# Seven half products for the gate and up tiles of the third feed-forward stage, and its hidden tile on GpSimd

## The reference, cut to what matters

```python
D_FF = 2816
def swiglu(x, w_gate, w_up, w_down):
    return (jax.nn.silu(x @ w_gate) * (x @ w_up)) @ w_down
for i in range(DEPTH):
    h = h + 0.5 * swiglu(rmsnorm(h, norm_ffn1[i]), ffn1_w_gate[i], ffn1_w_up[i], ffn1_w_down[i])
    ...                      # mixer, second feed-forward
    gate = jax.nn.sigmoid(rmsnorm(h, norm_ple[i]) @ w_ple_gate[i])
    h = h + gate * (p[i] @ w_ple_proj[i])
```

## Time and profile before

| | us |
|---|---|
| median of 3 runs | 3317.61 (3317.11 to 3319.28) |
| profiled execution | 3314.88 |
| its span, first to last instruction | 3313.6 |
| gate and up of stage 2 | 1084.05 to 1324.40 in the span |
| down of stage 2 | 1324.40 to 1444.08 |

### The profile page before, as it was taken

How to read it: one execution, slowest core, us unless ns; L and a number is a source line. 1 busy time by engine, 2 the same in 40 slices (tenths; PEclk the granted TensorE clock), 3 DMA queues, 4 the chain that set the end, 5 groups by cost and what they waited for, 6 DMA issues and landing times. The chain is left out here.

```text
span 3313.6 us, 46922 instructions
## 1 busy us (share of the span) xinstructions
PE 3213.5 (97%) x20296; PEld 2465.6 (74%) x20296; DVE 1528.2 (46%) x2218; ACT 1067.6 (32%) x1594; POOL 308.9 (9%) x365
## 2 busy tenths in 40 slices
PE   9999999999999999999999999979999999989988
PEld 7888887888888888889788888768877888424332
DVE  5443456644435544332754434685567544301112
ACT  4222226432223322322632223553344323200001
POOL 1000131200001000000210001211111301100000
PEclk9999999999999999999999999999999999999999
DMA  4222441122233222333222222301010323899998
GB/s 145 102 90 90 145 145 40 39 102 89 90 97 109 100 95 90 96 107 109 84 89 102 98 88 91 113 20 50 3 65 20 105 99 126 337 427 425 425 427 345
DMA packets 62798, 448.77 MB, mean 135 GB/s; under 512 B 8704, under 2 KB 10368, under 8 KB 32640
## 3 DMA queue, kind: packets, MB, share of 16 engines
q1 hardware_dynamic: 62592, 445.76, 36.0%
HBM read 438.39 MB, written 2.10 MB: 133 GB/s over the span
## 5 line engine op out<-in xcount | busy, mean ns | idle before, releaser
L568 DVE TENSOR_TENSOR w_lo<-slot,w_hi 128x2048 fp32r<-128x2048 f32 (+4 forms) x243 | 487.3, 2005 | 331.5 <-ACT w_hi L559 329.3
L167 PE MATMUL bank<-xa,w_hi 128*128 128x512 f32 x1368 | 535.7, 392 | 2.0 <-DVE w_lo L3162 2.0
L168 PE MATMUL bank<-xa,w_hi 128*128 128x512 f32 x1368 | 532.4, 389 | 0.0
L169 PE MATMUL bank<-xa,w_lo 128*128 128x512 f32 x1368 | 532.3, 389 | 0.0
L559 ACT ACTIVATE w_hi<-slot 128x2048 fp32r<-128x2048 f32 (+4 forms) x243 | 406.1, 1671 | 335.5 <-PE bank L169 327.0
L167 PE MATMUL bank<-xb,w_hi 128*128 128x512 f32 x832 | 324.7, 390 | 0.8 <-DVE w_lo L568 0.7
L169 PE MATMUL bank<-xb,w_lo 128*128 128x512 f32 x832 | 323.7, 389 | 0.0
L168 PE MATMUL bank<-xb,w_hi 128*128 128x512 f32 x832 | 323.7, 389 | 0.0
L167 PEld LDWEIGHTS bank<-xa,w_hi 128*128 128x128 f32 x1368 | 256.7, 188 | 63.1 <-issue 5.4
L168 PEld LDWEIGHTS bank<-xa,w_hi 128*128 128x128 f32 x1368 | 256.8, 188 | 53.9 <-issue 1.2
L169 PEld LDWEIGHTS bank<-xa,w_lo 128*128 128x128 f32 x1368 | 256.8, 188 | 53.7
(11 more groups left out here) (508 smaller groups left out, 4863.8 us busy)
## 6 DMA issues: line engine op xcount, KB each, us to landing
slot<-in_w_gu SPq DMA_DIRECT2D x87, 1024.0 KB, 4.8
slot<-in_exp_gate SPq DMA_DIRECT2D x25, 2048.0 KB, 15.1
slot<-in_exp_up SPq DMA_DIRECT2D x24, 2048.0 KB, 15.3
slot<-in_exp_down SPq DMA_DIRECT2D x24, 2048.0 KB, 15.8
slot<-in_w_dn SPq DMA_DIRECT2D x64, 704.0 KB, 4.0
slot<-in_w_gate SPq DMA_DIRECT2D x24, 768.0 KB, 4.3
xe<-in_exp_up SPq DMA_DIRECT2D x8, 2048.0 KB, 13.1
xe<-in_exp_down SPq DMA_DIRECT2D x8, 2048.0 KB, 15.2
```

Of the source, the lines that this page charges most:

```text
L167: e.matmul(out, w[0], x[0], start=(j == 0), stop=False)
L168: e.matmul(out, w[0], x[1], start=False, stop=False)
L169: return e.matmul(out, w[1], x[0], start=False, stop=(j == n - 1))
L568: dve.e.tensor_tensor(lo, slot(k, b), hi.bitcast(F32), ALU.subtract).then_inc(L.up("w_lo", b))
```

## The change

In stage 2 the gate and up tile is a product of 2 x 2 blocks: rows are gate and up, the inner sum is cut in two halves of 4 feature tiles, the 512 tokens in two halves of 256. It is made from 7 products (numbered 1 to 7, run in the order 1, 5, 2, 6, 7, 3, 4) of 4 feature tiles x 3 passes over 256 tokens: 84 matmuls of 256 columns instead of 48 of 512. Each of the 7 has a weight of 512 columns that is a block or a sum of blocks; each is split by ACT and DVE, into a ring of 8. The sums of weights are made by adding DMAs that POOL issues, but for one by DVE. 2 MB and not 1 MB are read from HBM per tile. x needs differences of its blocks too (made in the ple stage). DVE puts the 7 results together (`four`), POOL multiplies silu(gate) and up, and the split into `hid` is made for hidden tiles 0 to 9 during the last tile and for 10 to 21 behind it. `rstd` of the up half is applied in the down step, by one more DVE operation per output tile. The diff, cut to its core:

```diff
+SEVEN_ORDER = (1, 5, 2, 6, 7, 3, 4)
...
+def seven_free(k, f, s):
+
+    if s < 8:
+        return ("w_used", k.first[f"gu{f}"] - (2 if s < 4 else 1))
+    return ("seven", f, s - 8 if s < 152 else s - 4)
...
+def pe_seven(k, f, nm):
...
+        pe.wait_ge(*L.at("comb_lo", f, s))
+        for j in range(4):
+            c, t = slice(SEVEN_X[p] * 256, SEVEN_X[p] * 256 + 256), slice(j * P, (j + 1) * P)
+            x_lo, x_hi = cols(k.sv.x[j][:2], c)
+            pe.wait_ge(*L.at(SEVEN_READY[p], nm, j))
+            e.matmul(out, hi[:, t], x_hi, start=(j == 0), stop=False)
+            e.matmul(out, hi[:, t], x_lo, start=False, stop=False)
+            last = e.matmul(out, lo[:, t], x_hi, start=False, stop=(j == 3))
+        last.then_inc(L.up("seven", f, s))
+
+    for m in range(FF):
+        for p in SEVEN_ORDER:
+            product(p, m)
+            if m == 0 and p == 6:
+                pe_norm(k, nm)
...
+def pool_comb(k, f, m):
+
+    pool, L, b = k.pool, k.led, k.first[f"gu{f}"] + m
+    pool.wait_ge(*L.at("w_in", b))
+    pool.e.dma_start(k.sv.raw[m % 3][:, 1536:2560], k.order[b][0][:, 3072:4096], accum_op=ALU.add).then_inc(
+        L.up(f"raw_sum{m % 3}", b, by=16, also=[("w_sum", b)]), 16)
+    pool.wait_ge(*L.at("w_sum", b))
+    pool.e.dma_start(k.sv.pairs[m % 3], seven_raw(k, 5, m), accum_op=ALU.add).then_inc(
+        L.up(f"raw_sum{m % 3}", f"{b}", by=16, also=[("w_sum2", b)]), 16)
...
+def pool_hidden(k, f, m):
...
+    pool.wait_ge(*L.at("silu", f, m))
+    pool.wait_ge(*L.at("up_right", f, m))
+    pool.wait_ge(*L.at("ends", f, m))
+    pool.e.tensor_tensor(sv.hidden[m].rearrange("p (a c) -> p a c", a=2), ups, gates, ALU.mult).then_inc(L.up("hid_pool", f, m))
...
+        if layer == 0 and i == KT - 1:
+            for p in (1, 5, 2, 6):
+                dve_comb(k, SEVEN_FFN, p, 0)
...
-            dve_norm(k, nx, i, gain, k.xa)
+            dve_seven_x(k, nx, i)
...
+    pool_comb(k, SEVEN_FFN, 0)
+    pool_comb(k, SEVEN_FFN, 1)
     pool_norm(k, "n4")
+    for m in range(FF):
+        if m + 2 < FF:
+            pool_comb(k, SEVEN_FFN, m + 2)
+        pool_hidden(k, SEVEN_FFN, m)
```

More of the change, by code:

```diff
@@ L44 @@
 SIGNALS = {kind: sem for sem, kinds in {
+    "mixer_sums": "ple_gate ple_proj gate2 pool_mix branch rot qk_sum qk_spread seven",
+    "mixer_curves": "class_hi v_out p_hi edge_hi raw_in qk_sq qk_root yr_hi gate2_sigmoid mg_hi h_scaled",
+    "mixer_vectors": "ple_scaled ple_gated qk_part qk_scaled qk_inv qk_scale root_part root_sum gate2_scaled branch_gated merge_add mg_lo yr_lo p_lo",
+    "seven_curves": "comb_hi first_part x_f32 x1_hi x5_hi x2_f32 x23_hi x674_hi",
+    "seven_vectors": "comb_lo comb_sum gate_left two_more rest up_right ends gate_ready x5_diff x1_lo x5_lo x7_diff x6_diff x4_diff x23_lo x674_lo",
     "rwkv_sums": "kk_sum kk_spread low ysum bonus_sum ysq_sum y_spread g_sum",
@@ L235, in __init__, with plan_seven, area, block @@
         self.rb = [rb[:, i * P:(i + 1) * P] for i in range(3)] if rb is not None else [a.buf(P, "den_inv") for _ in range(3)]
+def plan_seven(k):
+    m, made = Kernel(), []
+    def area(start, size):
+        a = Arena(k.nc, start, made)
+        a.end = start + size
+        return a
+    def block(a):
+        b = a.copy()
+        return (a.buf(7 * 256, "xc_lo", F32R), a.buf(7 * 256, "xc_hi", F32R), b.buf(7 * 256, "x_low"), b.buf(7 * 256, "x_high"))
+    def pair(a):
+        b = a.copy()
+        return (a.buf(512, "comb_hi", F32R), a.buf(512, "comb_lo", F32R), b.buf(512, "comb_full"), b.buf(512, "comb_full"))[:4]
+    slots, parts, x, z = 3432, 11624, 19816, 28008
+    a = area(x, 8192)
+    m.x = [block(a), block(a)]
+    m.pairs = [a.buf(512, "raw7") for _ in range(2)] + [area(2880, 512).buf(512, "raw7")]
+    a = area(z, 12800)
+    b = a.copy()
+    hid_lo, m.hidden = [a.buf(512, "hid7_lo", F32R) for _ in range(FF)], [b.buf(512, "hidden") for _ in range(FF)]
+    m.four = a.buf(1024, "four")
+    m.first, m.two = a.buf(256, "first_part"), a.buf(256, "two_part")
+    a = area(z + 12800, 7168)
+    hid_late = [a.copy()]
+    m.x += [block(a), block(a)]
+    b = hid_late[0]
+    late = [b.buf(512, "hid7_hi", F32R) for _ in range(12)]
+    assert b.at <= a.at
+    m.raw = [a.buf(5 * 512, "raw7") for _ in range(2)]
+    b = area(a.at - 5120, 5120)
+    early = [b.buf(512, "hid7_hi", F32R) for _ in range(10)]
+    m.hid = [(hi, lo) for hi, lo in zip(early[5:] + early[:5] + late, hid_lo)]
+    a = area(slots + 1536, 2560)
+    m.raw += [a.buf(5 * 512, "raw7")]
+    a = area(parts, 8192)
+    m.ring = [pair(a) for _ in range(8)]
+    return m
 def plan_memory(k):
@@ L645, in pe_idle, with seven_raw @@
     last.then_inc(L.up("idle", name))
+SEVEN_ORDER = (1, 5, 2, 6, 7, 3, 4)
+SEVEN_BANK = {1: "one", 5: "mid", 2: "two", 6: "six", 7: "mid", 3: "end", 4: "end"}
+SEVEN_FREE = {"one": "first_part", "mid": "up_right", "two": "gate_left", "six": "two_more", "end": "ends"}
+SEVEN_X = {1: 0, 5: 1, 2: 2, 3: 3, 6: 4, 7: 5, 4: 6}
+SEVEN_READY = {1: "x1_lo", 5: "x5_lo", 2: "x23_lo", 3: "x23_lo", 6: "x674_lo", 7: "x674_lo", 4: "x674_lo"}
+SEVEN_RAW = {1: 0, 2: 512, 4: 1024, 7: 1536, 5: 2048}
+def seven_raw(k, p, m):
+    return k.sv.pairs[m % 3] if p == 6 else k.sv.raw[m % 3][:, SEVEN_RAW[p]:SEVEN_RAW[p] + 512]
@@ new lines, in act_hid_hi, with dve_hid_lo @@
+def act_hid_hi(k, f, j):
+    act, L = k.act, k.led
+    hi, lo = k.sv.hid[j]
+    act.wait_ge(*L.at("hid_pool", f, j))
+    act.wait_ge(*(L.at("comb_lo", f, seven_turn(4, FF - 2 if j < 5 else FF - 1)) if j < 10 else L.at("seven", f, 7 * FF - 1)))
+    act.e.activation(hi, k.sv.hidden[j], ACT.Copy).then_inc(L.up("hid_hi", f, j))
+def dve_hid_lo(k, f, j):
+    dve, L = k.dve, k.led
+    hi, lo = k.sv.hid[j]
+    dve.wait_ge(*L.at("hid_hi", f, j))
+    dve.e.tensor_tensor(lo, k.sv.hidden[j], hi.bitcast(F32), ALU.subtract).then_inc(L.up("hid_lo", f, j))
@@ new lines, in act_seven, with silu @@
+def act_seven(k, f, nm):
+    act, e, L, d0, sv = k.act, k.act.e, k.led, k.first[f"dn{f}"], k.sv
+    gates = sv.four.rearrange("p (a b c) -> p a b c", a=2, b=2)[:, :, 0, :]
+    def silu(m):
+        act.wait_ge(*L.at("gate_ready", f, m))
+        e.activation(gates, gates, ACT.Silu).then_inc(L.up("silu", f, m))
+    for p in (7, 3, 4):
+        act_comb(k, f, p, 0)
+    for m in range(FF):
+        more = m + 1 < FF
+        if more:
+            act_comb(k, f, 1, m + 1)
+        act.wait_ge(*L.at("seven", f, seven_turn(1, m)))
+        if m:
+            act.wait_ge(*L.at("two_more", f, m - 1))
+        e.activation(sv.first, k.banks.of("one", f, m)[:, 0:256], ACT.Copy).then_inc(L.up("first_part", f, m))
+        if more:
+            act_comb(k, f, 5, m + 1)
+        if m:
+            silu(m - 1)
+        if m == 0:
+            act_root(k, nm, k.rstd_last)
+        if more:
+            for p in (2, 6, 7, 3, 4):
+                act_comb(k, f, p, m + 1)
+        else:
+            for j in range(10):
+                act_hid_hi(k, f, j)
+                if j == 4:
+                    act_weight(k, d0)
+    silu(FF - 1)
+    act_weight(k, d0 + 1)
+    for j in range(10, FF):
+        act_hid_hi(k, f, j)
```

223 lines of the change are left out of this document (212 added, 11 removed).

## The result

| | before, us | after, us | ratio |
|---|---|---|---|
| median of the runs | 3318.45 (3317.11 to 3320.07, 4 runs) | 3369.57 (3368.41 to 3372.79, 4 runs) | 1.0155 [1.0138, 1.0173] |
| span of the profiled execution | 3313.6 | 3367.1 | |

Forecast were 3324.5 us and a range up to 3344: the time lies outside it. The direction was right, the size was not: 7 us slower forecast, 51 measured.

The account below looks back on a forecast made before the run. PE bounds the kernel now; after the change DVE's chain sets the pace. 3314.88 + 6.85 = 3321.7 us for the profiled execution, 3324.5 for a median, 0.21% slower; range 3311 to 3344.

Parts of the forecast that it names:

- PE's gain: Gate and up: 84 matmuls at 0.120 us make a tile 10.08 us, 0.84 less, 18.5 us over 22 tiles.
- Rival 3: Matmuls of 256 run 0.125 us apart, a tile 10.5: +5 us, 3329; counted inside the forecast's range and chance.
- DVE's step: Gate and up loop: a DVE step takes 10.26 us (10.15 to 10.5), slower than PE's 10.08, and PE follows it.
- waits until the other is through: DVE and POOL operations reading two SBUF inputs exclude each other; sharing instead would shorten the loop's first wait some 0.4 us.
- Rival 1: PE sets the pace if a DVE step is under 9.93 us: at 9.7, 3313, or 3309 with a cheaper entry; chance 0.23.
- The added DMAs: Gate and up loop: POOL's two sums per tile take 8 us together, hidden up to 10.6, so they cost nothing.
- D: Time from the issue of the first sum (512 KB) to the landing of the second (256 KB); taken as 8 us.
- rival 2: Adding DMAs set the pace, a step 5.0 + D / 2, from D = 10.5; 3337 at D = 11.8; chance 0.27.
- The page's fit: The skill's DMA price, 2.0 us plus bytes over 436 GB/s, gives 5.8 us for D, hidden too.
- The entry: Ple stage into gate and up: DVE's added x work delays PE, tile 0 ends at 1105.8, 10.8 us lost.
- The exit: Gate and up into down: PE starts 5.7 us late, loses another 3.0 at hid 10; the stage totals +6.85 us.
- Down and the c stage: One more DVE operation per down tile, +0.72 beside 15 us of matmuls; c stage margin 0.9 covers it: 0.

Follow-up runs that it names:

- e1: The changed kernel with POOL's adding DMAs and the waits for them left out, so no weight sums are formed: 3319.76 us, ratio 1.0004.
- e8: e1 (sums left out) with comb_sum moved ahead of rest, right behind comb 7, on DVE: 3321.80 us, ratio 1.0011.
- e2: The changed kernel with POOL's same two DMAs per tile as plain copies instead of adding, so no sum is formed: 3322.65 us, ratio 1.0011.
- e10: The changed kernel with only its second adding DMA (SBUF to SBUF, 256 KB) a plain copy: 3355.52 us, ratio 1.0116.
- e11: The changed kernel with POOL's four sums of tiles 0 and 1 laid between the norm's additions in the ple stage: 3361.68 us, ratio 1.0134.
- e9: Combined kernel (VectorE multiplying, second sum by POOL instruction, DVE and POOL entry reordered, comb_sum earlier) with the exit reordered: 3314.68 us, ratio 0.9991.
- e4: The changed kernel with VectorE, not POOL, multiplying silu(gate) and up; POOL only issues the sums: 3341.77 us, ratio 1.0071.
- e12: The changed kernel with SP's 1.5 MB load of tile t issued only when the second sum of tile t-2 has landed: 3350.18 us, ratio 1.0091.

## Why the prediction was wrong

**PE's gain: right.** In e1 1800 of its matmuls take 1320.84 - 1102.83 = 218.01 us, 0.121 each, with a wait of 1.0 in it; behind it the tiles are 10.08 us, as forecast. Rival 3 (0.125) did not come.

**DVE's step: right in size, a little high; that PE follows it, wrong.** 10.0 where nothing comes late, against 10.26 and the bound 10.15. The idle time before gate_left is 1.26 (forecast 1.5), that before comb 3 0.70 (0.7). Of the 0.26, 0.22 are ahead of gate_left, which starts 3.88 into a step and not 4.10: POOL's product starts as soon as the silu is there (1197.24, 2.16 into the step, beside comb 5), lasts 1.61 where one with DVE idle lasts 1.28, and is through at 3.77, 1.16 behind comb 5. That is less than a whole product behind it: the strict "waits until the other is through" comes out 0.1 us too long here, where full sharing was to take 0.4 off the wait; POOL's rows are rough, and nothing rests on it. Rival 1 asked for steps under 9.93; 10.0 lies just above. But PE's own tile is 10.08, so DVE is not the slower by a hair, as the forecast had it. Where no sum is late (e1), PE runs its tiles at 10.08 without a wait, and DVE, behind it by some 6 us at first, gains 0.08 a step. That is rival 1's path with hardly any of its gain: it asked for DVE to catch up, and the exit, which it had falling with DVE's lag, does not (e8).

**The added DMAs: the step that failed.** It said: "From hid_pool of step m (4.0) both must land and hi 6 be made before comb 6 of step m+1 at 5.05: D up to 10.6 is hidden. I take 8, hidden." The sign that the prediction named for its own failure, comb 6 waiting for the sum, is there ten times. The condition was right, and so, within 0.4 us, was rival 2's formula: by the landings D is 14.6 to 16.6 (15.3 in the mean) in every second tile and 10.9 to 13.3 in the others, past the 11.8 that I had as its end, and a long and a short step, 24.9 in the mean, are D and 9.6 us of fixed work, forecast 10.0. In the 20 steps this makes 40.2 us more than forecast. The mechanism stood in the text with 0.27; the price was wrong, in two ways. The rows behind it are of plain copies: adding takes the first from 4.8 to 6.5 or so, the second from 2.3 to 3.3, issuing on POOL included (e2, e10). And they are of nearly lone ones, though the same list had others of the same sizes, issued among further DMAs, that would have set a wider bound:

```profile
cos<-in_rope SPq DMA_DIRECT2D x2, 256.0 KB, 5.4
...
slot<-in_w_att SPq DMA_DIRECT2D x1, 512.0 KB, 8.6
```

I wrote that SP's 1.5 MB lie beside it, but took their mean over a step, when the load starts at one moment, the end of a step, and the second sum, 3.7 + 6.0 to 6.8 us into a step of 10.0, starts there too. That adds 5 us more, in which the sum's packets have not begun.

The page's fit of which I spoke (the Trainium skill, DMA: Bandwidth & Descriptors, Anatomy of one DMA) gave 5.8 for D. Lone plain copies took 3.7 (512 KB) and 2.3 (256 KB) in e2, 6.0 together, and so bear it out. In the loop, beside SP's load, it does not hold: measured are 7.4 for two plain copies, and for two adding ones 11.2 (1184.12 to 1192.04, and 3.3) and 15.1 in turn (8.4 behind 1180.84, from a first sum issued at 1174.12).

**The entry: half right.** Forecast were h(7) ready at 1095.0, x23_lo at 1098.8, x674_lo at 1100.0 and the first step of the loop at 1114.9; measured 1101.5, 1105.5, 1106.6 and 1121.0. They are 6.1 to 6.7 late, and the distances between them are right to 0.6. With the stall of the ple stage taken away (e11) they are at 1095.4, 1099.4, 1100.4 and 1114.9. The forecast had priced POOL's DMAs in the loop and not what stands behind them at their start: the norm's additions. The same mis-sizing is in it: the sums of two tiles, 7 to 8 us each, hold POOL from 1045 to 1060.

**The exit: right in size, in part by luck.** w_lo(d0) is ready 8.6 us into step 21 (forecast 8.15); PE waits 6.1 and 1.0 us (forecast 5.7 and 3.0). It is not the lag of DVE, as I had it, but the order of the last splits (e8, e9). Down itself takes 2.9 more: 1.0 is this wait, 2 the granted clock, 0.98 for 1.00. The clock was no term of the forecast; it makes up for the 2.0 by which the second wait was put too high.

**Down and the c stage: right** but for that clock. Forecast 0; behind the stage the two spans are the same (1869.5 us each).

The sum of the miss, 1497.64 against 1450.93 forecast for the start of the c stage, is 46.7: 6.1 at the entry, 40.2 in the 20 steps from 1121.02 to 1366.39 (245.4 for 205.2), 0.4 at the end.

Not settled: why the sum's packets do not start beside the load's. The trace shows that they don't, not by what rule. That sums which never leave behind a load would cost nothing (6.5 and 3.3 are 9.8 us for D, of which 10.6 are hidden) is worked out; in each kernel with both of them some meet it. Nor is it settled what the second half of the change, POOL's product, is worth by itself: undone alone (e4), the late sums decide, and whether by the buffers or by the meeting with the load is open.

## What to carry to other kernels

Price a DMA that adds as its own kind, and draw it on the time line of the step beside every large load: its latency is that of its place, here 3.3 or 8.5 us for the same 256 KB, and a mean bandwidth does not tell it; which of the two is issued first can decide. When a term has no row and rests on two prices of another kind, a bound of twice the nearest is no bound, and the slow rows of the same size belong beside the quick ones; a rival whose formula is sound and whose deciding point is near deserves the forecast's own weight. And when an idle engine is given new work, ask what that work delays where it starts, not only in its loop.

## What the runs showed of the hardware

- A DMA that adds, 512 KB from HBM: 5.4 and 5.5 us where no load was under way (issued at 1103.43 and 1348.60), 5.7 to 7.0 with SP's load issued 3.6 us before, 7.4 to 9.7 with the second sum under way too; plain 3.7, and 4.4 to 5.6 mostly behind the load. 256 KB within SBUF: 3.2 to 3.6, plain 2.3; 4.5 to 5.9 with a load issued 4 to 6 us before (e12). POOL is held 0.86 us by the issue, 0.54 to 0.58 by a plain one.
- Issued up to about 1 us behind SP's load of 1.5 MB, or up to 0.4 us ahead of it, the same 256 KB take 7.8 to 9.5, plain 6.2 to 7.4 us, and their first packet starts 4.0 to 5.8 us behind the issue and not 1.1 to 1.4. Issued 0.5 to 1.7 us ahead, plain ones take 2.2 to 2.7 (e2).
- Sums hold the DMA engines for longer: for less moved the share is larger. The windows 1100 to 1300 of the whole change, e1, e2 and e4, in this order:

```profile
1100.00:1300.00 200.00, 176.20 (x1361) 173.39 (x1361) 134.25 (x229) 81.67 (x152) 51.02 (x47) 0.94 0.73 186
```
```profile
1100.00:1300.00 200.00, 198.26 (x1643) 197.41 (x1644) 159.77 (x276) 96.82 (x184) 30.44 (x19) 1.00 0.45 154
```
```profile
1100.00:1300.00 200.00, 195.60 (x1619) 194.37 (x1618) 158.13 (x272) 93.77 (x178) 49.69 (x56) 1.00 0.64 226
```
```profile
1100.00:1300.00 200.00, 187.81 (x1535) 185.54 (x1535) 161.48 (x277) 91.08 (x170) 31.66 (x36) 1.00 0.81 209
```

  186 GB/s at a share of 0.73 with sums, 226 at 0.64 with copies.
- The same rows show the clock: 0.94 granted in the whole change, where PE stood for up to 4.5 us at a time in the long steps, 1.00 in the other three. Behind some of these waits (the one of 4.5 us among them; behind one of 3.5 at 1166.02 not) PE ran at 1.2 GHz for a few us, its matmuls of 256 columns 0.213 apart and not 0.120:

```profile
1342.59 0.41 PE L771 MATMUL bank<-xc_hi,comb_hi 128*128 128x256 f32 x1
1342.80 0.41 PE L772 MATMUL bank<-xc_lo,comb_hi 128*128 128x256 f32 x1
```

  It cost little: the short steps behind are 10.0 as in e1, and DVE has no wait for PE in the stage.
